# Moving the sum of the fourth neighbourhood head tile's squares one tile later in block 1

## What is computed

```python
p = h @ w_in                                   # cq, ckv, kr, and na = q, k, v of 8 heads of 64
mq = (rms_norm(c_q, g_qa) @ w_uq)              # 8 heads of 96
kv = (rms_norm(c_kv, g_kva) @ w_ukv)           # k_nope and mv of 8 heads
mk = rms_norm(concat([k_nope, k_rope]), g_mk)
nq = rms_norm(na[:, :, 0], g_nq)               # the neighbourhood heads: mean of squares over 64
nk = rms_norm(na[:, :, 1], g_nk)
nv = na[:, :, 2]
# then dense attention on mq, mk, mv; neighbourhood attention on nq, nk, nv; gated merge; MLP
```

## Time and profile before

| | |
|---|---|
| median of 3 runs | 1857.26 us (1856.57 to 1858.93) |
| the profiled execution | 1859.92 us, of which its span is 1857.8 us |
| TensorE busy | 1820.9 us, 98% of the span |
| VectorE, ScalarE busy | 1316.7 us (71%), 944.3 us (51%) |
| chain that ended last | 90% TensorE, 4% VectorE, 3% ScalarE |
| mean granted TensorE clock | 0.998 |

### The profile page before, as it was taken

How to read it: one execution, slowest core, us unless ns; L and a number is a source line. 1 busy time by engine, 2 the same in 40 slices (tenths; PEclk the granted TensorE clock), 3 DMA queues, 4 the chain that set the end, 5 groups by cost and what they waited for, 6 DMA issues and landing times.

```text
span 1857.8 us, 29195 instructions
## 1 busy us (share of the span) xinstructions
PE 1820.9 (98%) x11286; PEld 1562.2 (84%) x11286; DVE 1316.7 (71%) x2387; ACT 944.3 (51%) x1760; POOL 28.4 (2%) x57
## 2 busy tenths in 40 slices
PE   8999999999999999999999999999999999999998
PEld 6777556788888888889785899999999989999887
DVE  6765676688898888866568677666676775676674
ACT  4344565653432232336446675554464764564763
POOL 0000000000000000000000000000000000000000
PEclk9999999999999999999999999999999999999999
DMA  7432301245355554423223245555454425455423
GB/s 309 133 114 77 122 24 69 102 170 170 104 225 184 206 199 181 181 91 123 68 81 135 109 172 205 184 185 190 154 184 161 136 83 180 160 179 167 131 92 125
DMA packets 55720, 272.47 MB, mean 147 GB/s; under 512 B 6432, under 2 KB 6688, under 8 KB 38432
## 3 DMA queue, kind: packets, MB, share of 16 engines
q1 hardware_dynamic: 47952, 225.40, 34.8%
q0 software_dynamic: 7632, 45.21, 6.9%
HBM read 269.53 MB, written 1.05 MB: 146 GB/s over the span
## 4 chain that ended last, share of the span: by engine, by line
PE 90%; DVE 4%; ACT 3%; DMA 1%; issue 1%; SPq 0%; DVEq 0%; ACTq 0%
PE bank L631 22%; PE bank L633 21%; PE bank L632 21%; PE bank L994 3%; PE bank L1002 2%; PE bank L791 2%; PE bank L679 1%; PE bank L667 1%; PE bank L1099 1%; DMA wide<-in_ada 1%; DVE w_parts L2181 1%; PE bank L736 1%; PE bank L749 1%; PE bank L1320 1%; PE bank L1321 1%
## 5 line engine op out<-in xcount | busy, mean ns | idle before, releaser
L2194 DVE TENSOR_TENSOR small_lo<-ring,small_hi 128x1024 fp32r<-128x1024 f32 (+1 forms) x192 | 227.5, 1194 | 134.7 <-ACT small_hi L1588 132.5
L631 PE MATMUL bank<-h_hi,small_hi 128*128 128x256 f32 (+3 forms) x992 | 308.6, 311 | 1.8 <-DVE h_lo L2330 1.4
L633 PE MATMUL bank<-h_hi,small_lo 128*128 128x256 f32 (+3 forms) x992 | 299.9, 302 | 0.0
L632 PE MATMUL bank<-h_lo,small_hi 128*128 128x256 f32 (+3 forms) x992 | 299.2, 302 | 0.0
L1573 ACT ACTIVATE w_parts<-ring 128x1024 fp32r<-128x1024 f32 x192 | 201.3, 1051 | 163.2 <-PE bank L633 163.2
L632 PE MATMUL bank<-h_parts,w_parts 128*128 128x256 f32 (+1 forms) x784 | 260.5, 332 | 0.0
L2181 DVE TENSOR_TENSOR w_parts<-ring,w_parts 128x1024 fp32r<-128x1024 f32 x192 | 233.2, 1218 | 20.9 <-ACT w_parts L1573 20.8
L632 PE MATMUL bank<-b_parts,w_parts 128*128 128x256 f32 (+1 forms) x656 | 217.2, 331 | 0.0
L1588 ACT ACTIVATE small_hi<-ring 128x1024 fp32r<-128x1024 f32 (+1 forms) x192 | 194.2, 1028 | 30.1 <-PE bank L1339 16.0
L631 PEld LDWEIGHTS bank<-h_hi,small_hi 128*128 128x128 f32 (+2 forms) x992 | 185.6, 187 | 15.0 <-issue 4.6
L632 PEld LDWEIGHTS bank<-h_lo,small_hi 128*128 128x128 f32 (+2 forms) x992 | 184.7, 186 | 10.4 <-issue 2.2
(11 more groups left out here) (353 smaller groups left out, 3902.1 us busy)
## 6 DMA issues: line engine op xcount, KB each, us to landing
ring<-in_w SPq DMA_DIRECT2D x204, 512.0 KB, 3.5
ring<-in_w SPq DMA_DIRECT2D x96, 1024.0 KB, 4.8
lowrank<-in_rows POOLq DMA_DIRECT2D x24, 1024.0 KB, 5.1
prob<-in_rows POOLq DMA_DIRECT2D x24, 512.0 KB, 3.8
wide<-in_ada SPq DMA_DIRECT2D x8, 1024.0 KB, 8.8
ring<-in_w SPq DMA_DIRECT2D x14, 384.0 KB, 3.2
lowrank<-in_bias POOLq DMA_DIRECT2D x2, 2048.0 KB, 11.7
x<-in_x SPq DMA_DIRECT2D x2, 1024.0 KB, 9.9
```

The source lines that it names most:

```text
L631: pe.matmul(ps, w[0][:, k, :], hi, start=k == 0, stop=False)
L632: pe.matmul(ps, w[0][:, k, :], lo, start=False, stop=False)
L633: return pe.matmul(ps, w[1][:, k, :], hi, start=False, stop=k == nk - 1)
L2194: dve.tensor_tensor(small_lo[:, slot, 0:size], small[:, slot, 0:size], rounded(i)[:, 0:size].bitcast(F32), ALU.subtract).then_inc(*signal( ...
```

## The change

In three loops the steps of the fourth tile move. These are `nq` and `nk` in layer 0 and `nk` in layer 1; in layer 1's `nq` loop the sum already stands one tile later. In layer 0 the fourth sum of `nq` goes behind the first `nk` tile, as that loop's `behind`. In both layers the fourth sum of `nk` goes behind mk0, past krot and before nv0. ScalarE's `head_rms` and VectorE's `scale_head` move along.

```diff
 def project_heads(name, c0, behind=None):
-    for i in range(5):
-        if i < 4:
-            project(name, i, c0)
+    for i in range(4):
+        project(name, i, c0)
         if i == 0 and behind:
             behind()
-        if i and not (behind and i == 4):
+        if i:
             head_sum(name, i - 1, l, TT - c0)
...
                     project_heads("nq", t0)
+                    project_heads("nk", 0, lambda: head_sum("nq", 3, l, cw))
                 else:
...
-                project_heads("nk", 0)
+                    project_heads("nk", 0)
                 pe.wait_ge(*event("kr_gain", l))
                 rotate(("krot", l), slice(NOPE, QK), krope[NOPE:QK, 2, TC:TT], ("krot_sin", l))
                 for i in range(NH + 1):
...
                         full(split_linear(ps[:, :], ("uk", l, i // 2), ckv_hi, ckv_lo, ("ckv_lo", l)), "mk", l, i // 2)
+                    if i == 0:
+                        head_sum("nk", 3, l, TT)
                     if i % 2:
                         head_sum("mk", i // 2, l, TT)
...
+                    projected_heads("nk", 0, lambda: head_rms("nq", 3, t0))
...
                         square(("mk", i // 2), l, 0, 1, bank(("mk", l, i // 2))[:, :])
+                    if i == 0:
+                        head_rms("nk", 3, 0)
...
+                    projected_heads("nk", 0, lambda: scale_head("nq", 3, t0))
...
                     if i == 0:
                         low_cq(5)
+                        scale_head("nk", 3, 0)
```

More of the change, by code:

```diff
@@ L1699, in projected_heads @@
                 def projected_heads(name, c0, behind=None):
-                    for i in range(5):
+                    for i in range(5 if name == "nk" else 4):
                         if name == "nk" and i < 2:
@@ L1709, in projected_heads @@
                             behind()
-                        if i and not (behind and i == 4):
+                        if 0 < i < 4:
                             head_rms(name, i - 1, c0)
@@ L1736, in _ @@
                     rms("ckv", l, KVL, P, TT, ("normed", "ckv", l, 1))
-                projected_heads("nk", 0)
+                    projected_heads("nk", 0)
                 def key_rms(i):
```

## The result

The changed kernel takes 1863.68 us, the median of 7 runs (1862.89 to 1864.98). The kernel before took 1858.93 us on the same chip (median of 7, 1856.57 to 1859.37). The ratio is 1.0028, with a 95% interval of 1.0018 to 1.0037: slower by little, but clear of no change. On the median given at the start (1857.26) the ratio makes 5.2 us, with an interval of 3.3 to 6.9; forecast were 6.0.

What follows compares the result with a forecast made beforehand. TensorE, busy for 1820.9 of 1857.8 us, was taken to bound the kernel. Gain -2.6, waits +6.0 and clock +2.6 gave +6.0 us on 1857.3, so 1863.3 us; range 1859.8 to 1865.2.

Steps and rivals of the forecast that it cites:

- the gain: Three fourth sums on TensorE no longer wait for ScalarE's square: 2.6 us in all, bounds 2.0 and 2.8.
- 0.89 + 0.85: Gains in layer 0: 0.89 us at `nq`, 0.85 at `nk`; layer 1's `nk` was also given 0.85.
- the 0.91 that the forecast took for the places: Gain per `nk` loop reckoned by places: 1.86 us go before krot, 0.95 come back behind mk0; 0.83 by the wait.
- The wait: nv3 gets mk0's bank and waits until VectorE has scaled mk0's second head: 3.0 us per layer, 6.0 in all.
- 0.14: Time in us from an event, here the end of mk0's second head's scaling, to TensorE's start on nv3.
- The clock: TensorE's clock falls at both nv3 waits, costing 1.3 us per layer, 2.6 in all; forecast's chance 0.50.
- this 1.70: Upper bound of one clock fall: the full-clock time in us missing from 28 to 33 us in the profile before.
- mk2's own 0.07: mk2's first matmul took 0.30 us instead of 0.23 before; this 0.07 goes, against about 0.06 for beginning again.
- the rival with one fall: Clock falls at only one of the two nv3 waits: +4.7 us, 1862.0; chance 0.20.
- the rival without any: Clock holds at full through both nv3 waits: +3.4 us, 1860.7; chance 0.18.
- took the delay up later: Rival: a later wait, on a transfer, absorbs 1.5 us at most; about +2.5 without the clock, 1859.8; chance 0.05.
- ScalarE's logarithm at its new place: Moved between mk0's square and nv0's copy; costed at nothing, as an nv tile's 2.97 us on TensorE covers it.

Runs made afterwards that it cites:

- the bank kept: Changed kernel, but the fourth `nk` sum's bank is taken ahead of krot's, in the old order; 1856.12 us, ratio 0.9983 to the kernel before.
- The keys scaled first: Changed kernel, but VectorE scales mk0's second head right behind the first, ahead of the weights' rest; 1856.44 us, ratio 0.9988 to the kernel before.
- the filled kernel: Changed kernel plus 8 matmuls of 192 columns that nobody reads, ahead of nv3; 1861.66 us, ratio 1.0014 to the kernel before.
- the wait alone: Kernel before, nothing moved, but krot and mk0 take their banks ahead of the fourth `nk` sum; 1867.63 us, ratio 1.0047 to the kernel before.
- `nq` alone: Kernel before with only layer 0's `nq` loop changed, both `nk` loops as before; 1856.97 us, ratio 0.9991 to the kernel before.
- the half filled wait: Changed kernel plus 4 matmuls of 192 columns that nobody reads, ahead of nv3; 1860.57 us, ratio 1.0013 to the kernel before.

## Why the prediction was right

**The bound, and the gain.** TensorE bounds the kernel, and the three sums no longer wait. From the third `nk` sum to nv0's second matmul, layer 1 took 4.88 us before (913.59 to 918.47) and takes 3.98 after (913.38 to 917.36): 0.90 where 0.85 stood. In layer 0, with `nq` in it, the third `nq` sum to mk0's sum took 33.83 and takes 32.03 (110.72 to 142.75): 1.80 where 0.89 + 0.85 stood. Gain 2.7 for 2.6. Inside the 0.91 that the forecast took for the places, two errors cancel: krot begins 0.96 behind the third sum and not 0.87 (136.03 to 136.99), and the sum behind mk0 takes 0.85 and not 0.95 (139.03 to nv0's second matmul at 140.00, less one matmul of 0.12). The kernel with the bank kept shows it by runs: 3.2 us, from 1.5 to 4.8.

**The wait.** It came at the instruction named, from the releaser named, for the reason named. From mk1's sum to nv3 it was 1.38 us in layer 1 before (929.85 to 931.23) and is 4.33 after (928.72 to 933.05): 2.95, forecast 3.0. nv3 began 0.05 us behind the end of the scaling in layer 0 and not 0.14, which accounts for the difference. The keys scaled first took it away, and the old kernel with the new order of banks got it in full.

**The clock.** It fell at both waits, the half of the chances that went to the forecast. From nv3 to mk2's sum it was 7.29 us before (931.23 to 938.52) and is 8.71 after (933.05 to 941.76): 1.42 per layer, forecast 1.3. The loss in PEclk is 1.70 a layer (0.10 + 0.24 of 5 us in layer 0, 0.08 + 0.26 in layer 1), as much as in the earlier trace rows. The forecast took less than this 1.70 because part of the low stretch might lie in the wait itself. That reason was wrong: the clock is full until nv3 has started, and the whole low stretch lies behind the wait. What keeps the price below 1.70 is another thing. At the low clock matmuls of 256 columns begin 0.214 us apart (13 of them from 156.27 to 159.05 in layer 0) instead of 0.12, 1.8 times and not twice as far, which leaves 1.5 of the 1.70. And mk2's own 0.07, which the forecast counted with the wait, is gone: from nv3 to mk2's sum the filled kernel takes 7.22 (155.52 to 162.74) where 7.29 stood. So the price came out near 1.3 partly by luck. The Trainium skill ("TensorE: Matmul & The Clock Gate", Part 1 on the HAM clock gate) has the clock low unless activity lifts it; the runs here agree, for the filled hole kept 1.00 and the bare one did not.

**The sum.** Layer 0 by its own rows: -1.80 + 2.93 + 1.44 = 2.57, as measured (nv3 from 1.39 to 4.32 behind mk1's sum, mk2's sum from 7.29 to 8.73 behind nv3). Layer 1: -0.90 + 2.95 + 1.42 = 3.47, measured 3.44. The forecast of 6.0 for both was right to 0.1, but partly because small errors cancel: 0.1 too little gain and 0.1 too much wait against 0.3 too little for the clock.

**What the runs alone would not have told.** Measured medians differ by 4.75, which is the rival with one fall (4.7) to the digit, and the interval of 3.3 to 6.9 holds the rival without any (3.4) too. Only the profile separates them: PEclk is low behind both waits. Part of the scatter that hides this is of the same kind: in the profiles of these kernels a fall to about 0.66 over 5 us comes near 28 us (before, the bank kept, the wait alone), near 218 (the filled wait, `nq` alone) or near 1762 (the bank kept, the half filled wait), and in those of the changed kernel and of keys first at none of these places. Each takes about 1.7 us of full clock and none belongs to the change. Near 28 us the three with a fall are those in which TensorE had waited longest for a transfer shortly before (1.22 to 1.25 us; 0.86 at most in the others). At the other two places the wait ahead is the same in all eight; why the fall comes and goes there was not tried.

**The other rivals.** Nothing took the delay up later: of the 6.0 us that the two stretches lost, what lies between and behind them gave back 0.2 at most (742.69 to 742.64 us from mk2's sum in layer 0 to the second `nk` sum in layer 1, 919.3 to 919.1 from mk2's sum in layer 1 to the end). ScalarE's logarithm at its new place did not make a bank late, as no other line of waits appeared.

## What to carry to other kernels

Moving one instruction also moves its turn at whatever is handed out in program order: here the bank passed on was worth 8.7 us and the move itself 2.7 to 3.2 the other way. Before such a move, list who holds each buffer now and later, and until which event; where one holder is long, hand the buffers out in the old order. On an engine that sets the pace, price a hole of about 3 us with its after-effect on the clock, here half as much again; where it could not be closed, work that nobody reads kept the clock here.

## What the runs showed of the hardware

All four bare holes of 2.87 us (two in the changed kernel, two in the old one with the new banks) were followed by a low clock: 0.76, 0.74, 0.66 and 0.73 over the 5 us stretch that holds most of it. The two of 1.4 us and the two filled ones at the same place were followed by 1.00. Elsewhere the same wait went both ways: the clock fell behind 1.90 us in two profiles of eight and behind 1.41 us in two of eight. Unexpected was where the loss stands: in layer 0 of the changed kernel the granted clock is still 1.00 in the microsecond in which the hole ends, and 0.50, the level of 1.2 GHz, in the three behind it, while TensorE is busy throughout. A stretch of these traces that shows a low clock and a fully busy engine is thus to be explained by what lies ahead of it. And the products that filled the hole cost nothing that shows: nv3 began 4.33 us behind mk1's sum with them and 4.32 without.
